# A transformer block on one core: rows behind the second norm turned by VectorE in 32x32 squares instead of by TensorE

## The chip, the cores and the metric

The kernel runs on one core of one Trainium2 chip. A core has five engines that run their own instruction lists and meet at semaphores: TensorE (PE), VectorE (DVE), ScalarE (ACT), GpSimd (POOL) and SyncE (SP, which here only issues DMAs), and 16 DMA engines. The metric is the device time of one execution in microseconds (us), as the median of several.

## The reference

The input is x, 2048 tokens of 1024 features, f32. The block computes

```
u = rmsnorm(x, ln1_g);  proj = u @ w_in            # 2816 columns: a_q a_f a_i a_g | b_q b_k b_v
y_a = hgrn2_mixer(...)                             # 4 heads, gated linear recurrence in chunks of 64
y_b = swa_sink_attention(...)                      # 8 heads, window 128, sinks, ALiBi
h = x + concat(y_a, y_b) @ w_out
u = rmsnorm(h, ln2_g)                              # "the second norm"
h = h + (silu(u @ w_gate) * (u @ w_up)) @ w_down   # 2816 hidden columns
out = rmsnorm(h, final_g)
```

Everything is f32. Precise products are made from pairs: each operand is split into a rounded high part and the rest (`hi`, `lo`), and a product is three matmuls, hi x hi, hi x lo, lo x hi.

## The kernel before

**Mixers.** The tokens are taken in NSB = 4 blocks of T = 512 (`it` = 0 to 3, TB = 4 rows of 128 tokens each). Each engine runs `slots(it)`, 27 slots, and then `out_b(it)`. In slots 0 to 21 TensorE makes one group: 128 columns of `w_in` against u, 8 x 3 matmuls of 128x512 (`group`, L971 to 973). Into the slots a fixed plan puts the small steps: attention step i = 0 to 15 has its scores in slot i+2, its sum in i+3, its turn (`p_turn`) in i+4 and its product with the values in groups of four in slots 8, 12, 16, 20. Recurrence head a has its four groups from slot F_SLOT = (4, 9, 14, 18) on; three slots behind the first come its `iv` turn and key product (`iv_turn`, `keys`), four behind it the turn of its key and the update (`key_turn`, `update`), five behind the output (`output_inside`, L1148, which waits for the last of eight states that VectorE makes in `update`, L1953), six behind the norm. In slots 22 to 26 and in `out_b` TensorE multiplies by `w_out` in units 22 to 29, four k-pairs for the left half of the columns (banks M) and four for the right (banks X). `w_in` and `w_out` are split once, in iteration 0, and stored to `w_scr` as 1 MB units; later iterations load unit n into one of three places (`split`, `split_next`) as soon as unit n-3 has been used (`load_split`, L642). VectorE makes the splits of iteration 0 too (`make_lo`), with GpSimd in some slots.

**The second norm and its turn.** Block it-1's h is kept as four tiles of 128 tokens x 1024 and is scaled in iteration it, slots 12 to 15 (`h_scale`, L2162). The FFN wants it with the features on the partitions. So in slots 18 to 25 of iteration it TensorE turns it, half a row tile (`j` = 0 to 7) a slot: `u_turn` makes four 128x128 transposes into bank X[0] (L1186), ScalarE copies the bank to a tile of four buffers (`u_out`, L1469), and SP stores the tile to `u_scr[it, partition, feature group, token]` (`store_u`, L661). The eight halves of the last block are turned in the FFN, in four pairs behind the products named in `U_LAST`, through X[2] and X[3]. `s_ftr` counts the turns, `s_uev` the copies, `s_us[0..3]` the stores. The rows of x for the residual are loaded over the freed h tiles (`load_rows`, L619), in SP's order `u 3, r 0, r 1, u 4, unit 26, u 5, r 2, u 6, unit 27, u 7, r 3, unit 28, unit 29`; in the last iteration the operand loads stand between these too (`load_operand`, L712).

**FFN.** It is a Strassen-Winograd product over pairs of blocks (NPAIR = 2): operands B11, B21, T1 to T4, B22 are loaded from `u_scr` or combined and split; 22 groups of 7 products of 12 matmuls 128x512 (`ffn_product`, L1282 to 1284), whose weights ScalarE and VectorE split three products ahead (LEAD = 3, L1649 and L2180); and then `down`, 77 rows of 12 matmuls (L1307 to 1309), fed by a ring of four buffers.

**Order around the change.** Every engine works strictly in the order written. SP waits for a semaphore ahead of nearly every DMA, so a late store holds all loads behind it.

Of the kernel before, what the change touches and what calls it, by code (L numbers as in the profile page):

```python
# [94 lines left out]
POOL_LOW = (8, 9, 13, 14, 17, 18, 22)  # L95
COMBINE_AT = {27: 0, 37: 1, 39: 2, 48: 3}
SPLIT_AT = {50: "B11", 52: "T2", 54: "T1", 59: "T3", 61: "B21", 63: "T4", 65: "B22"}
GAIN_AT = (63, 64, 65, 70)
T_LOAD = 9
U_LAST = ((5, 6), (6, 3), (6, 6), (7, 3))  # L100
# [37 lines left out]
def block_program(nc, x, ln1_g, w_in, lb_logits, hgrn_norm_g, attn_sinks, attn_norm_g, w_out, ln2_g,  # L138
# [31 lines left out]
    u_scr = nc.dram_tensor("u_scr", [NSB, P, KD, T], F32, kind="Internal").ap()  # L170
# [6 lines left out]
    with ExitStack() as ctx:  # L177
# [188 lines left out]
        def wait_u_stored(eng, it, j=7):  # L366

            for n in range(4):
                eng.wait_ge(s_us[n], 32 * it + 16 * ((j - n) // 4 + 1))
# [155 lines left out]
        s_ftr = sem("s_ftr")  # L525
# [74 lines left out]
        def _(sp):  # L600
# [12 lines left out]
            def load_rows(it, b):  # L613

                if it == NSB - 1 and b < 2:
                    sp.wait_ge(s_ptr0, NSB * 2 * TB)
                elif it:
                    sp.wait_ge(s_ftr, (it - 1) * 2 * TB + 2 * b + 2)
                sp.dma_start(x_rows(it, b)[:, :], x_t[it * TB + b, :, :]).then_inc(s_xh[b], 16)  # L619
# [37 lines left out]
            def store_u(it, j):  # L657
# [3 lines left out]
                sp.dma_start(u_scr[it, :, 4 * half:4 * half + 4, b * P:(b + 1) * P],  # L661
                             u_tile(it, j)[:, :].rearrange("p (c t) -> p c t", c=4)).then_inc(s_us[j % 4], 16)
# [22 lines left out]
            def load_operand(p, o, part=None):  # L685
# [22 lines left out]
                if p == 0 and o == B22:  # L708
                    sp.wait_ge(s_ftr, (NSB - 2) * 2 * TB + 4)
# [256 lines left out]
        def _(pe):  # L966
# [48 lines left out]
            def group(it, slot):  # L1015
# [5 lines left out]
                for k in range(KD):  # L1021
                    last = product(M[slot % 3][:, :], place_of(it, slot), uhi[:, k, :], ulo[:, k, :], k,
# [144 lines left out]
            def u_turn(it, j):  # L1167

                b, half = divmod(j, 2)
                if it == NSB - 1:  # L1170
                    bank = X[2 + half]
                    pe.wait_ge(s_u, it * TB + j + 1)
                    if j >= 2:
                        pe.wait_ge(s_uev, it * 2 * TB + j - 1)
                    else:
                        pe.wait_ge(s_h, NSB * KD)
                else:
                    bank = X[0]
                    pe.wait_ge(s_u, it * TB + b + 1)
                    if j:  # L1180
                        pe.wait_ge(s_uev, it * 2 * TB + j)
                    else:
                        pe.wait_ge(s_bias, (it + 1) * STEPS + STEPS)
                for c in range(4):
                    k = 4 * half + c
                    last = tr(bank[:, c * P:(c + 1) * P], h_of(it)[b][:, k * P:(k + 1) * P], ident[:, :])  # L1186
                last.then_inc(s_ftr, 1)

            def slots(it):

                for slot in range(SLOTS):
                    if slot < IN_GROUPS and (it or slot >= 2):
                        group(it, slot)
# [36 lines left out]
                    if it and 0 <= slot - UT_SLOT < 2 * TB:  # L1230
                        u_turn(it - 1, slot - UT_SLOT)
# [56 lines left out]
            def ffn(p):  # L1288
                for g in range(NG):
                    for o in range(PRODUCTS):  # L1290
                        ffn_product(p, g, o)
                        if p == 0 and (g, o) in U_LAST:
                            u_turn(NSB - 1, 2 * U_LAST.index((g, o)))
                            u_turn(NSB - 1, 2 * U_LAST.index((g, o)) + 1)

# [58 lines left out]
        def _(act):  # L1354
# [105 lines left out]
            def u_out(it, j):  # L1460
                act.wait_ge(s_ftr, it * 2 * TB + j + 1)
                if j >= 4:
                    act.wait_ge(s_us[j % 4], 32 * it + 16)
                elif it == NSB - 1:
                    act.wait_ge(s_group, NSB * UNITS)
                else:
                    act.wait_ge(s_score, (it + 1) * STEPS + STEPS)
                    act.wait_ge(s_u, (it + 1) * TB)
                A(u_tile(it, j)[:, :], X[0 if it < NSB - 1 else 2 + j % 2][:, :], ACT.Copy).then_inc(s_uev, 1)  # L1469

# [27 lines left out]
            def slots(it):  # L1498
                for slot in range(SLOTS):
# [23 lines left out]
                    if slot in Q_SLOT:  # L1523
# [3 lines left out]
                        elif it >= 2:  # L1527
                            for par in range(2):
                                act.wait_ge(s_us[2 * p + par], 32 * (it - 1))
# [28 lines left out]
                    if it and 0 <= slot - UT_SLOT < 2 * TB:  # L1558
                        u_out(it - 1, slot - UT_SLOT)
# [91 lines left out]
            def ffn(p):  # L1651
                for g in range(NG):
                    G, j = NG * p + g, NJ * p + g // 2
                    x, y, z = banks_of(p, g)
                    for o in range(PRODUCTS):
# [35 lines left out]
                        if p == 0 and PRODUCTS * g + o - 1 in [PRODUCTS * x + y for x, y in U_LAST]:  # L1691
                            for half in range(2):
                                u_out(NSB - 1, 2 * [PRODUCTS * x + y for x, y in U_LAST].index(PRODUCTS * g + o - 1) + half)
# [98 lines left out]
        def _(dve):  # L1792
# [102 lines left out]
            def head_group(it, a, part, bank):  # L1895
# [22 lines left out]
                if part in (1, 2):  # L1918
                    half = slice((part - 1) * (T // 2), part * (T // 2))
                    dve.wait_ge(s_cum, n + 1)  # L1920
                    if a:
# [672 lines left out]
```

## Time and profile before

| | us |
|---|---|
| Median of 3 runs | 2169.23 (2168.64 to 2169.85) |
| The profiled execution's own time | 2167.59 |
| Its span, first to last instruction | 2165.9 |
| TensorE busy | 2134.2 (99%) |
| VectorE busy | 1364.3 (63%) |
| ScalarE busy | 843.6 (39%) |
| GpSimd busy | 432.5 (20%) |
| DMA queue of SP, share of 16 engines | 54.6%, 400.63 MB |

How to read it: a busy TensorE is not TensorE at its peak, since its matmuls overlap and their ends are modelled; the distance from start to start is what a matmul costs. The mixers take from 0 to about 890 us, iterations 1 to 3 some 174 us each, and the rest is the FFN. Idle time of an engine other than TensorE costs nothing by itself.

### The profile page before, as it was taken

How to read it: one execution, taken by the hardware profiler on the slowest of the kernel's cores; microseconds unless marked ns; L12 is line 12 of the kernel's file. 1: busy time of each engine (PE TensorE's matmuls, PEld its weight loads, DVE VectorE, ACT ScalarE, POOL GpSimd, SP SyncE). 2: the span in 40 equal slices, each digit the busy share in tenths (PEclk: the TensorE clock that was granted, in tenths of full speed). 3: DMA queues.
4: the chain of work that ended last, by engine and by line, in shares of the span. 5: the costliest groups of instructions: out<-in, count | busy, mean ns of one | idle time of the engine just before them, and what ended most of it. 6: DMA issues, size and time to landing. Idle time of an engine off the chain costs nothing.

```text
span 2165.9 us, 28872 instructions
## 1 busy us (share of the span) xinstructions
PE 2134.2 (99%) x10708; PEld 1778.9 (82%) x10708; DVE 1364.3 (63%) x2136; ACT 843.6 (39%) x1628; POOL 432.5 (20%) x403
## 2 busy tenths in 40 slices
PE   8999999999999999999999999999999999999998
PEld 7878888888888888788888887888888888888886
DVE  5886477547754776766566765568755556564556
ACT  5343342324232423444333333356433333333445
POOL 2342022102210221222233230000222233210000
PEclk9999999999999999999999999999999999999999
DMA  7666754664467437543355657887433323237666
GB/s 247 227 231 209 264 183 145 198 223 179 146 196 229 171 132 235 217 148 115 107 209 214 218 191 234 261 267 253 172 101 102 106 89 122 93 105 236 225 208 228
DMA packets 215740, 402.48 MB, mean 186 GB/s; under 512 B 16944, under 2 KB 100912, under 8 KB 211760
## 3 DMA queue, kind: packets, MB, share of 16 engines
q1 hardware_dynamic: 215600, 400.63, 54.6%
q8 instruction: 86, 1.41, 0.3%
q14 instruction: 54, 0.44, 0.1%
HBM read 292.04 MB, written 108.53 MB: 185 GB/s over the span
## 4 chain that ended last, share of the span: by engine, by line
PE 87%; DVE 5%; issue 4%; DMA 2%; ACT 1%; POOL 1%; SPq 0%; DVEq 0%; ACTq 0%; POOLq 0%
PE M L1282 10%; PE M L1284 10%; PE M L1283 10%; PE M L971 6%; PE M L973 6%; PE M L972 6%; PE M L1307 3%; PE M L1309 3%; PE M L1308 3%; PE X L1309 3%; PE X L1308 3%; PE X L1307 3%; PE X L1284 3%; PE X L1282 3%; PE X L1283 3%
## 5 line engine op out<-in xcount | busy, mean ns | idle before, releaser
L2292 DVE TENSOR_TENSOR ring_lo<-ring_raw,ring_hi 128x1024 fp32r<-128x1024 f32 x154 | 189.7, 1232 | 162.6 <-ACT ring_hi L1707 162.1
L1707 ACT ACTIVATE ring_hi<-ring_raw 128x1024 fp32r<-128x1024 f32 x154 | 163.3, 1061 | 230.4 <-DMA ring_raw<-a_scr 225.5
L1282 PE MATMUL M<-t_hi,wu_hi 128*128 128x512 f32 x616 | 240.2, 390 | 0.3 <-DVE wu_lo L2180 0.3
L1284 PE MATMUL M<-t_hi,wu_lo 128*128 128x512 f32 x616 | 239.9, 390 | 0.0
L1283 PE MATMUL M<-t_lo,wu_hi 128*128 128x512 f32 x616 | 239.7, 389 | 0.0
L971 PE MATMUL M<-uhi,split 128*128 128x512 f32 (+1 forms) x528 | 206.6, 391 | 2.9 <-DVE ulo L1843 2.9
L973 PE MATMUL M<-uhi,split 128*128 128x512 f32 (+1 forms) x528 | 202.9, 384 | 0.0
L972 PE MATMUL M<-ulo,split 128*128 128x512 f32 (+1 forms) x528 | 202.4, 383 | 0.0
L2180 DVE TENSOR_TENSOR wu_lo<-fraw,wu_hi 128x512 fp32r<-128x512 f32 x132 | 124.0, 948 | 123.3 <-ACT wu_hi L1649 122.9
L2557 POOL TENSOR_TENSOR fs<-fraw 128x512 f32<-128x512 f32 x43 | 61.0, 1418 | 415.8 <-DMA fraw<-in_w_gate_dram 208.5
L2477 POOL TENSOR_TENSOR pr<-pr,rd 128x256 f32<-128x256 f32 x64 | 44.6, 697 | 459.1 <-DVE rd L1854 459.1
L1282 PEld LDWEIGHTS M<-t_hi,wu_hi 128*128 128x128 f32 x616 | 115.6, 188 | 25.0 <-DVE wu_lo L2180 1.1
L1283 PEld LDWEIGHTS M<-t_lo,wu_hi 128*128 128x128 f32 x616 | 115.8, 188 | 24.1
L1284 PEld LDWEIGHTS M<-t_hi,wu_lo 128*128 128x128 f32 x616 | 115.6, 188 | 24.1
L2563 POOL TENSOR_TENSOR fraw<-fraw,fs 128x512 f32<-128x512 f32 x43 | 55.9, 1300 | 369.1 <-DVE wl_lo L2180 369.1
L1307 PE MATMUL M<-ring_hi 128*128 128x512 f32 x308 | 120.4, 391 | 2.3 <-DVE ring_lo L2292 2.3
L1308 PE MATMUL M<-ring_lo,ring_hi 128*128 128x512 f32 x308 | 119.9, 389 | 0.0
L1309 PE MATMUL M<-ring_hi,ring_lo 128*128 128x512 f32 x308 | 119.9, 389 | 0.0
L1307 PE MATMUL X<-ring_hi 128*128 128x512 f32 x308 | 119.8, 389 | 0.0
L1309 PE MATMUL X<-ring_hi,ring_lo 128*128 128x512 f32 x308 | 119.8, 389 | 0.0
L1308 PE MATMUL X<-ring_lo,ring_hi 128*128 128x512 f32 x308 | 119.8, 389 | 0.0
L971 PEld LDWEIGHTS M<-uhi,split 128*128 128x128 f32 x528 | 99.3, 188 | 23.9 <-issue 5.1
(312 smaller groups left out, 5012.6 us busy)
## 6 DMA issues: line engine op xcount, KB each, us to landing
split<-w_scr SPq DMA_DIRECT2D x60, 1024.0 KB, 5.6
ring_raw<-a_scr SPq DMA_DIRECT2D x154, 256.0 KB, 3.6
w_scr<-split SPq DMA_DIRECT2D x30, 1024.0 KB, 6.5
split_next<-w_scr SPq DMA_DIRECT2D x30, 1024.0 KB, 5.0
fraw<-in_w_gate_dram SPq DMA_DIRECT2D x44, 512.0 KB, 4.8
fraw<-in_w_up_dram SPq DMA_DIRECT2D x44, 512.0 KB, 4.8
a_scr<-au SPq DMA_DIRECT2D x88, 256.0 KB, 2.4
ring_raw<-t_scr SPq DMA_DIRECT2D x88, 256.0 KB, 3.0
```

The costliest lines, as they stand in the source:

```text
L971: mm(bank, whi[s][:, kb, :], hi, start=first, stop=False)
L972: mm(bank, whi[s][:, kb, :], lo, start=False, stop=False)
L973: return mm(bank, wlo[s][:, kb, :], hi, start=False, stop=last)
L1282: mm(bank[:, :], wh[:, k, :], hi[:, k, :], start=start and k == 0, stop=False, skip_group_check=True)
L1283: mm(bank[:, :], wh[:, k, :], lo[:, k, :], start=False, stop=False, skip_group_check=True)
L1284: last = mm(bank[:, :], wl[:, k, :], hi[:, k, :], start=False, stop=k == KH - 1, skip_group_check=True)
L1307: mm(bank[:, :], hi[:, 1, tokens], hi[:, 0, :], start=first, stop=False, skip_group_check=True)
L1308: mm(bank[:, :], hi[:, 1, tokens], lo[:, 0, :], start=False, stop=False, skip_group_check=True)
L1309: done = mm(bank[:, :], lo[:, 1, tokens], hi[:, 0, :], start=False, stop=last, skip_group_check=True)
L1707: A(hi[:, :, :], raw_r[:, :, :], ACT.Copy).then_inc(s_rowhi, 1)
L2180: V.tensor_tensor(wl[:, :, :], ffn_part(p, g, o), wh[:, :, :].bitcast(F32), ALU.subtract).then_inc(s_flo, 1)
L2292: V.tensor_tensor(lo[:, :, :], raw_r[:, :, :], hi[:, :, :].bitcast(F32), ALU.subtract).then_inc(s_rowlo, 1)
```

## The change

1. `u_turn` (TensorE) and `u_out` (ScalarE) go. In their slots VectorE makes one `transpose` of a half tile, 128 tokens x 512 features, straight from h (`u_blocks`). It turns each 32x32 square by itself: token 32i+t, feature 32n+c comes to partition 32i+c, column 32n+t.
2. The squares are put in order by the stores. `u_scr` becomes `[NSB, 32, KD, 4, T]`, and `store_u` makes four DMAs, one for each 32 tokens, in runs of 32 tokens, 128 bytes; before it was one DMA with runs of 128 tokens, 512 bytes. The semaphores `s_us` count four times as far. `load_operand` reads rows of T tokens (2048 bytes), as before, in the new order.
3. `s_ftr` goes: the loads into freed h tiles, and of B22, wait for `s_uev`, which VectorE now raises. `out_b` waits for the last scores of bank X[0] and not for the last copy of u.
4. `key_turn` of heads 0 to 2 moves from behind the group of its slot (8, 13, 18) into the middle of it, between k = 3 and k = 4. Head 3's stays in slot 22.
5. On VectorE the reciprocal of the decay (`inverse`, parts 1 and 2 of a head) moves to the front of its slot, ahead of the scores; in slots 5, 9, 13, 17 (`UNFOLD_LAST`) the masked copy of the turned probabilities (`unfold`, L1892) moves behind the head's keys, update and norm.

```diff
-    u_scr = nc.dram_tensor("u_scr", [NSB, P, KD, T], F32, kind="Internal").ap()
+    u_scr = nc.dram_tensor("u_scr", [NSB, P // 4, KD, 4, T], F32, kind="Internal").ap()
...
-                eng.wait_ge(s_us[n], 32 * it + 16 * ((j - n) // 4 + 1))
+                eng.wait_ge(s_us[n], U_PARTS * (32 * it + 16 * ((j - n) // 4 + 1)))
...
                 elif it:
-                    sp.wait_ge(s_ftr, (it - 1) * 2 * TB + 2 * b + 2)
+                    sp.wait_ge(s_uev, (it - 1) * 2 * TB + 2 * b + 2)
...
-                sp.dma_start(u_scr[it, :, 4 * half:4 * half + 4, b * P:(b + 1) * P],
-                             u_tile(it, j)[:, :].rearrange("p (c t) -> p c t", c=4)).then_inc(s_us[j % 4], 16)
+                for i in range(U_PARTS):
+                    tokens = slice(b * P + 32 * i, b * P + 32 * i + 32)
+                    sp.dma_start(u_scr[it, :, 4 * half:4 * half + 4, :, tokens].rearrange("c k m t -> c (k m) t"),
+                                 u_tile(it, j)[32 * i:32 * i + 32, :].rearrange("c (n t) -> c n t", n=16)
+                                 ).then_inc(s_us[j % 4], 16)
...
-                    sp.dma_start(OPERAND[o][2][:, k, :], u_scr[2 * p + n, :, k0 + k, :]).then_inc(s_opl[o], 16)
+                    sp.dma_start(OPERAND[o][2][:, k, :], u_scr[2 * p + n, :, k0 + k, :, :].rearrange("c m t -> m c t")
+                                 ).then_inc(s_opl[o], 16)
...
-            def group(it, slot):
+            def group(it, slot, head=None):
...
                 for k in range(KD):
+                    if head is not None and k == KD // 2:
+                        key_turn(it, head)
...
-                for c in range(4):
-                    k = 4 * half + c
-                    last = tr(bank[:, c * P:(c + 1) * P], h_of(it)[b][:, k * P:(k + 1) * P], ident[:, :])
-                last.then_inc(s_ftr, 1)
...
-                    a = head_at(slot, UPDATE)
-                    if a is not None and slot != OUT_A:
-                        key_turn(it, a)
...
-                        if c == 0 and bank == 0 and it:
-                            pe.wait_ge(s_uev, it * 2 * TB)
+                        if c == 0 and bank == 0:
+                            pe.wait_ge(s_bias, (it + 1) * STEPS)
...
-                A(u_tile(it, j)[:, :], X[0 if it < NSB - 1 else 2 + j % 2][:, :], ACT.Copy).then_inc(s_uev, 1)
...
+                    a, part = head_part(slot)
+                    if part in (1, 2):
+                        inverse(it, a, part)
...
-                        unfold(it, i)
+                        if slot not in UNFOLD_LAST:
+                            unfold(it, i)
...
+                    if slot in UNFOLD_LAST:
+                        unfold(it, step_at(slot, P_TURN))
...
+                    if it and 0 <= slot - UT_SLOT < 2 * TB:
+                        u_blocks(it - 1, slot - UT_SLOT)
...
+            def u_blocks(it, j):
+                b, half = divmod(j, 2)
+                dve.wait_ge(s_u, it * TB + (j if it == NSB - 1 else b) + 1)
+                if j >= 4:
+                    dve.wait_ge(s_us[j % 4], U_PARTS * (32 * it + 16))
+                elif it == NSB - 1:
+                    dve.wait_ge(s_group, NSB * UNITS)
+                else:
+                    dve.wait_ge(s_score, (it + 1) * STEPS + STEPS)
+                    dve.wait_ge(s_u, (it + 1) * TB)
+                V.transpose(u_tile(it, j)[:, :], h_of(it)[b][:, half * T:(half + 1) * T]).then_inc(s_uev, 1)
...
+                        if p == 0 and (g, o) in U_LAST:
+                            for half in range(2):
+                                u_blocks(NSB - 1, 2 * U_LAST.index((g, o)) + half)
```

## Rows read from the trace of the kernel before

**Rows 1.** The page, part 1: busy us, share, instructions of each engine.

```profile
PE 2134.2 (99%) x10708; PEld 1778.9 (82%) x10708; DVE 1364.3 (63%) x2136; ACT 843.6 (39%) x1628; POOL 432.5 (20%) x403
```

**Rows 2.** Waits of TensorE, whole run: us in total, times, longest.

```profile
PE X L1148 <- DVE st L1953: 5.7, 5, 1.8
...
PE X L1124 <- POOL key L2466: 2.8, 3, 2.1
PE X L1141 <- ACT kst L1415: 2.7, 4, 0.7
```

**Rows 3.** Windows: us, busy by engine, PEclk, DMA share, GB/s.

```profile
862.00:884.00 22.00, 21.96 (x99) 17.84 (x97) 17.29 (x12) 8.31 (x6) 0.00 (x0) 1.00 1.05 398
424.00:446.00 22.00, 22.00 (x112) 18.46 (x111) 10.32 (x14) 5.77 (x11) 0.00 (x0) 1.00 0.77 265
```

**Rows 4.** Groups of TensorE by line: busy us, mean ns | idle before.

```profile
L1186 PE MATMUL X<-ident,h 128*128 128x128 f32 x96 | 15.2, 281 | 0.0
...
L1186 PE MATMUL X<-ident,h_last 128*128 128x128 f32 x32 | 4.1, 272 | 0.0
```

**Rows 5.** Timeline of TensorE, iteration 1, slot 22: start, us.

```profile
406.33 0.39 PE L979 MATMUL M<-split,yhi 128*128 128x512 f32 x1
...
406.79 0.39 PE L981 MATMUL M<-split,yhi 128*128 128x512 f32 x1
407.02 0.60 PE L1132 MATMUL X<-ident,forget 128*128 128x128 f32 x4
...
407.69 0.40 PE L980 MATMUL M<-split,ylo 128*128 128x512 f32 x1
```

**Rows 6.** Groups of VectorE by line: a copy of a whole tile.

```profile
L2032 DVE COPY oT<-M 128x512 f32<-128x512 f32 x16 | 11.0, 685 | 3.6 <-PE M L1099 3.6
```

**Rows 7.** Timelines of four engines, iteration 1, slots 13 to 18.

```profile
341.95 1.22 DVE L1892 TENSOR_TENSOR pT<-X,keep 128x1024 int32<-128x1024 int32 x1
...
345.79 0.49 PE L1148 MATMUL X<-iv,amask 128*128 128x128 f32 x2 [0.83 <-DVE st L1953]
...
349.45 0.54 DVE L1900 TENSOR_SCALAR forget<-forget,f_mul,f_add 128x512 f32<-128x512 f32 x1
...
373.84 0.58 ACT L1409 ACTIVATE iv<-X 128x512 f32<-128x512 f32 x1
...
377.74 0.49 PE L1141 MATMUL X<-iv,kst 64*128 64x128 f32 x4 [0.69 <-ACT kst L1415]
```

**Rows 8.** Timeline of all engines, iteration 1, slots 22 and 23.

```profile
412.53 0.35 DVE L1953 SCALAR_TENSOR_TENSOR st<-state,cum,X 128x128 f32<-128x128 f32 x1 [0.46 <-PE X L1141]
...
415.56 1.05 PE L1148 MATMUL X<-iv,amask 128*128 128x128 f32 x8
```

**Rows 9.** Timelines, iteration 0 (slots 7, 8) and iteration 1 (slot 7).

```profile
70.61 1.16 PE L1124 MATMUL X<-qdec,key 128*128 128x128 f32 x8 [2.11 <-POOL key L2466]
...
74.61 0.58 ACT L1409 ACTIVATE iv<-X 128x512 f32<-128x512 f32 x1
...
291.80 0.58 ACT L1409 ACTIVATE iv<-X 128x512 f32<-128x512 f32 x1
```

**Rows 10.** DMA at 124.1 to 126, then 13.0 to 14.6: packets, MB, share.

```profile
q1 hardware_dynamic: 728, 0.37, 71.6%
...
q1 hardware_dynamic: 1788, 0.03, 65.9%
```

**Rows 11.** Timeline of SP, iteration 3: issues of units 26, 28, a tile.

```profile
855.48 0.53 SPq L642 DMA_DIRECT2D split<-w_scr  x1
...
864.21 0.45 SPq L661 DMA_DIRECT2D u_scr<-uthird  x1
...
867.75 0.53 SPq L642 DMA_DIRECT2D split<-w_scr  x1
```

**Rows 12.** DMA issues at 867.6 to 867.9: count, KB, us to landing.

```profile
split<-w_scr SPq DMA_DIRECT2D x1, 1024.0 KB, 10.8
```

**Rows 13.** Timeline of TensorE, iteration 3: the first matmul of unit 28.

```profile
878.63 0.50 PE L979 MATMUL X<-split,yhi 128*128 128x512 f32 x1
```

More of the change, by code:

```diff
@@ L95 @@
 POOL_LOW = (8, 9, 13, 14, 17, 18, 22)
+UNFOLD_LAST = (5, 9, 13, 17)
 COMBINE_AT = {27: 0, 37: 1, 39: 2, 48: 3}
@@ L99 @@
 T_LOAD = 9
+U_PARTS = 4
 U_LAST = ((5, 6), (6, 3), (6, 6), (7, 3))
@@ L524, in block_program @@
         s_fo = sem("s_fo")
-        s_ftr = sem("s_ftr")
         INI, DST = 10, 4
@@ L708, in load_operand @@
                 if p == 0 and o == B22:
-                    sp.wait_ge(s_ftr, (NSB - 2) * 2 * TB + 4)
+                    sp.wait_ge(s_uev, (NSB - 2) * 2 * TB + 4)
                     sp.wait_ge(s_u, (NSB - 1) * TB)
                 for k in range(KH) if part is None else (part,):
-                    sp.dma_start(OPERAND[o][2][:, k, :], u_scr[2 * p + n, :, k0 + k, :]).then_inc(s_opl[o], 16)
+                    sp.dma_start(OPERAND[o][2][:, k, :], u_scr[2 * p + n, :, k0 + k, :, :].rearrange("c m t -> m c t")
+                                 ).then_inc(s_opl[o], 16)
             def store_a(p, j, n):
@@ L1165, in head_turn @@
                 last.then_inc(s_amul, 1)
[L1167 to L1183, printed above, removed]
-                for c in range(4):
-                    k = 4 * half + c
-                    last = tr(bank[:, c * P:(c + 1) * P], h_of(it)[b][:, k * P:(k + 1) * P], ident[:, :])
-                last.then_inc(s_ftr, 1)
             def slots(it):
@@ L1192, in slots @@
                     if slot < IN_GROUPS and (it or slot >= 2):
-                        group(it, slot)
+                        group(it, slot, head_at(slot, UPDATE))
                     for k in A_PLAN.get(slot, ()):
@@ L1229, in slots @@
                             step(it, a)
-                    if it and 0 <= slot - UT_SLOT < 2 * TB:
-                        u_turn(it - 1, slot - UT_SLOT)
             def out_b(it):
@@ L1291, in ffn @@
                         ffn_product(p, g, o)
-                        if p == 0 and (g, o) in U_LAST:
-                            u_turn(NSB - 1, 2 * U_LAST.index((g, o)))
-                            u_turn(NSB - 1, 2 * U_LAST.index((g, o)) + 1)
             def down(p):
@@ L1458, in swa_hi @@
                 A(yhi[:, HEADS + p, :], oT[p][:, :], ACT.Copy).then_inc(s_ybhi, 1)
[L1460 to L1468, printed above, removed]
-                A(u_tile(it, j)[:, :], X[0 if it < NSB - 1 else 2 + j % 2][:, :], ACT.Copy).then_inc(s_uev, 1)
             def h_square(it, b):
@@ L1528, in slots @@
                             for par in range(2):
-                                act.wait_ge(s_us[2 * p + par], 32 * (it - 1))
+                                act.wait_ge(s_us[2 * p + par], U_PARTS * 32 * (it - 1))
                         for par in range(2):
@@ L1557, in slots @@
                             step(it, a)
-                    if it and 0 <= slot - UT_SLOT < 2 * TB:
-                        u_out(it - 1, slot - UT_SLOT)
                     if 0 <= slot - X_SCALE < 2 and it + 1 == NSB:
@@ L1690, in ffn @@
                             h_root(NSB - 1)
-                        if p == 0 and PRODUCTS * g + o - 1 in [PRODUCTS * x + y for x, y in U_LAST]:
-                            for half in range(2):
-                                u_out(NSB - 1, 2 * [PRODUCTS * x + y for x, y in U_LAST].index(PRODUCTS * g + o - 1) + half)
                         if g == NG - 1 and o == S3:
@@ L1917, in head_group @@
                                            op0=ALU.mult, op1=ALU.mult).then_inc(s_qdec, 1)
[L1918 to L1921, printed above, removed]
-                        dve.wait_ge(s_key, 2 * n)
-                    V.reciprocal(cuminv[:, half], cum[w][:, half]).then_inc(s_inv, 1)
                 if part == 3:
@@ L1927, in head_group, with inverse @@
                                            op0=ALU.add, op1=ALU.mult).then_inc(s_gs, 1)
+            def inverse(it, a, part):
+                n = it * HEADS + a
+                half = slice((part - 1) * (T // 2), part * (T // 2))
+                dve.wait_ge(s_cum, n + 1)
+                if a:
+                    dve.wait_ge(s_key, 2 * n)
+                V.reciprocal(cuminv[:, half], cum[a % 2][:, half]).then_inc(s_inv, 1)
             def keys(it, a):
```

## The prediction

> **What bounds the kernel now.** I read first the page's busy shares: TensorE is busy in 99% of the span and VectorE in 63%, so only what takes time off TensorE's queue, or puts a wait into it, moves the end [rows 1]. The second view is TensorE's list of waits over the whole run: about 20 us in all, of which VectorE's state chain, GpSimd's key and ScalarE's `kst` copy hold 11.2 us, all inside the mixers [rows 2]. The third is the DMA share by stretches: where iteration 1 moves its stores of u, from 424 to 446 us, the 16 DMA engines have room (share 0.77), but in the last mixer iteration they are full, at 1.05, from 862 to 884 us [rows 3], and that is where I expect this change to be decided.
>
> **Terms on TensorE.** The change takes 96 + 32 square turns off TensorE [rows 4]. Four turns (of another tile, the same shape) alone between big matmuls are seen from 406.79 to 407.69: from the big matmul before them to the second one behind them 0.90 us pass, where two steps of big matmuls take 0.46 (406.33 to 406.79), so four turns cost 0.44 us [rows 5]. Behind other small matmuls four turns take about the same. 32 groups of four: 32 x 0.44 = **14.1 us gained**. ScalarE's 32 copies of the turned tiles go too; ScalarE is at 39% [rows 1] and no wait of TensorE is for them [rows 2], so that is worth nothing by itself.
>
> **Terms on VectorE.** It gets 32 square turns of 128x512 f32. No such row exists. The nearest are a plain copy of that size, 0.685 us [rows 6], and below it a scalar operation, 0.54; above it stands the masked unfold of 128x1024, 1.22 us [rows 7]. I take 0.7 and keep 0.54 and 1.22 for the range; the difference only delays SP by half a microsecond a tile. The Trainium skill (page "VectorE: DVE Perf Modes", section "The three transpose paths") gives 311 ns for a 128x128 bf16 piece in 32x32 squares, by which four would take an estimated 1.24 us; no run here shows it yet, and by that price VectorE would do 0.5 us more per tile. In slots 18 to 21 the new work falls into VectorE's idle time, since VectorE waits for TensorE in each of them; the last eight lie in the FFN, where VectorE's weights are made three products ahead (LEAD), 36 big matmuls of 0.23 us, 8 us. So the turns themselves cost nothing on the path. Only their lateness does, through SP (below).
>
> In slot 22 the gain is not kept. TensorE does the update first, VectorE then makes eight states one behind the other from 412.53 to 415.56, and TensorE begins L1148 at 415.56, which is to say it already arrives with nothing to spare [rows 8]. With the turn between them gone it arrives 0.4 us sooner and waits 0.4 us longer: **-1.2 us** for three iterations.
>
> **The key's turn and the new order on VectorE.** In slot 14 of each iteration TensorE waits 0.83 us for the last state; VectorE did the unfold (1.22 us) ahead of the states, at 341.95 [rows 7]. With the unfold behind them, and ScalarE's `qs` copy 0.6 us sooner, since `kst` is out of its way, that wait goes; ScalarE and GpSimd behind it have moved by only 0.6, so I count 0.6 x 3 = **1.8 us**. In slot 18 TensorE waits 0.69 us for `kst` [rows 7]. Now the key is turned after half the group, near 373.9, but the turn needs the bank that ScalarE's `iv` copy reads, and that copy runs at 373.84 to 374.42. So a wait of up to 0.6 can take the place of the 0.69. It can also vanish, since the order of VectorE and GpSimd ahead of that copy moves. Bounds 0 and 0.69 x 3; I take **1.4 us**.
>
> Iteration 0 is another matter, since VectorE also splits weights there. The reciprocal now stands ahead of the scores, so in slots 6 and 7 the scores, ScalarE's exponentials and the `iv` copy come up to 1.74 us later. Before, `iv` was copied at 74.61, and TensorE had just lost 2.11 us waiting for the key [rows 9]. After: no wait for the key, TensorE at the half of group 8 at 72.2, `iv` ready near 76.9, then 0.4 for the turn and 2.7 for the second half: 80.1 where it was 77.5 before, -2.6. Against that, the 1.8 us wait of iteration 0 in slot 14 goes; slot 18 costs perhaps 0.7 in the same way. Together **-1.5 us**, between -5 and +5.
>
> **The DMA queue.** A tile of u left in 512 pieces of 512 bytes and now leaves in 2048 pieces of 128, from four issues instead of one. A stretch with only 512-byte packets gives 0.716 x 16 x 1.9 us / 728 = 29.9 ns each; one with 1,788 packets in 0.03 MB, 17 bytes each on average, gives 0.659 x 16 x 1.6 / 1788 = 9.4 ns [rows 10]. So a tile takes 512 x 29.9 / 16 = 0.96 us of all engines now, and after the change between 2048 x 9.4 / 16 = 1.2 and 2048 x 29.9 / 16 = 3.8 us. A straight line between the rows gives 14.5 ns; the tiny packets were reads and these are writes to DRAM, so I take 18 ns: 2.3 us, **1.35 us more per tile**. Four issues of 0.45 us cost SP 1.8 us instead of 0.45 [rows 11]. The loads of operands read the same 2048-byte rows as before and cost nothing new.
>
> In iterations 1 and 2 the stretch of these stores has the engines at 0.77 of full [rows 3], and the next weights have several us to spare. Iteration 3 has not. SP issues the weights of unit 28 at 867.75, they take 10.8 us and land at 878.6, and TensorE begins on them at 878.63 [rows 11 to 13]: it is already held by that load. The engines are full up to there, so whatever is put ahead of that load delays it one for one. Ahead of it, since the load of unit 26 at 855.48, stand three tiles of u (the last at 864.21): + 3 x 1.35 = 4.0. The backlog starts somewhat sooner: TensorE is ahead by four turns and the `kst` wait (2.4 us), VectorE ends its slot 22 at 852.0, turns the fifth tile until 852.7, SP issues it four times until 854.5, and then issues unit 26, 1.0 us sooner than before. Landing: 878.6 - 1.0 + 4.0 = 881.6. TensorE would be there at 878.6 - 2.4 - 3 x 0.44 = 874.9. So **a new wait of 6.7 us** (bounds by the piece's price: 3.4 at 9.4 ns, 11.3 at 29.9 ns). The first FFN weights stand behind it in the same queue and in VectorE's, so it isn't won back.
>
> In iterations 1 and 2 SP issues x's rows of block 3 behind the last tile of u, and TensorE's next turns of x need the bank that they free. They come some 3 us later, and TensorE gets there 3 us sooner (seven turns); I count that as just fitting, at nothing.
>
> **Sum.** 14.1 - 1.2 + 1.8 + 1.4 - 1.5 - 6.7 = 7.9 us. The profiled execution took 2167.6 (span 2165.9 and 1.7 around it), 1.6 under the median of 2169.2: 2159.7 there, **2161.3 us** as a median.
>
> **The rivals.**
> *Small pieces are as dear as large ones* (29.9 ns). Iteration 3 waits 11.3, and in iterations 1 and 2 the row of block 3 and unit 28 come about 2.5 us late each. 14.1 - 1.2 + 3.2 - 1.5 - 11.3 - 5 = -1.7: 2170.9. For it: from 4096 to 512 bytes the price per byte already rises. Against it: a tiny packet takes a third of that. Chance 0.20.
>
> *The stores become the bound* (the other side). If a piece costs twice a 512-byte packet, 60 ns, a tile takes 7.7 us. Iteration 3 waits 878.6 - 1.0 + 20 - 874.9 = 22.8, iterations 1 and 2 some 12 each, after the room of 5 us is used: -32 us, 2200. It decides from about 28 ns per piece up, where the sum is nothing. Chance 0.08. The Trainium skill (page "DMA: Bandwidth & Descriptors", section "Specifications") says that below 512 bytes the engines do a read-modify-write, which would be such a doubling; no store to DRAM in this kernel has pieces under 512 bytes, so no row bears it out or excludes it.
>
> *The transfers are hidden anyway.* If the queue isn't what holds unit 28, only 14.1 - 1.2 + 3.2 - 1.5 = 14.6 is left: 2154.6. For it: a tile's stores could drain while SP is still issuing, beside the loads. Against it: the share of 1.05 and a landing 0.04 us ahead of the matmul. Chance 0.18.
>
> *The key's turn within the group makes waits of its own.* ScalarE's `iv` copy is ready only 0.65 us ahead of the half of group 8 (its copy at 291.80 takes 0.58, and the half is near 293.05) [rows 9]. If the new order makes it 1 us late in slots 8 and 18 of three iterations and iteration 0 loses 5, then 7.9 - 1.4 - 3 - 3.5 = 0: 2169. Chance 0.12.
>
> **How the numbers follow.** The forecast has 0.42 and by itself 2157 to 2166. A change of 0.2%, 4.3 us, is about what a measurement of this kernel can tell from none. Faster by more (under 2164.9): most of the forecast, 0.38, the hidden transfers, 0.18, and 0.06 of the others, 0.62. Within: 0.20, from the dear pieces, the key's waits and the forecast's end. Slower: 0.18, all of the store-bound case and half of the dear pieces. The range, 2153 to 2174, leaves out the store-bound case and the tails.
>
> **What the profile after would show.** L1186's and L1469's rows gone and TensorE's busy time about 14 us lower; a turn of 128x512 on VectorE at 0.7 us; packets under 512 bytes up by 65,536 and their mean share; unit 28's matmuls in iteration 3 behind a wait of 3 to 11 us; the 0.83 us wait in slot 14 gone; a wait of TensorE for `iv` at the half of group 8 in iteration 0. The prediction is wrong if a tile's stores take 5 us or more to land in a quiet stretch, or if iterations 1 and 2 also show TensorE waiting for weights.

## The result and the profile after

The changed kernel takes 2242.77 us (median of 5, 2239.54 to 2244.64), the one before 2169.85 in the same measurement (2168.64 to 2171.34): ratio 1.0338, 95% interval 1.0326 to 1.0350. It is slower by 73 us; 2161.3 with a range of 2153 to 2174 was forecast.

The page of the changed kernel, busy us, share and instructions of each engine, and the packets:

```profile
PE 2144.0 (96%) x10580; PEld 1771.0 (79%) x10580; DVE 1379.6 (62%) x2168; ACT 828.2 (37%) x1596; POOL 427.1 (19%) x403
...
DMA packets 265755, 402.47 MB, mean 180 GB/s; under 512 B 83344, under 2 KB 150928, under 8 KB 261776
```

Against [rows 1], TensorE's 128 turns are gone, but its busy time rose by 9.8 us instead of falling. A busy time that grows with fewer instructions asks for the granted clock. Windows of the changed kernel in iteration 3 (us, busy by engine, granted clock, DMA share, GB/s):

```profile
862.00:884.00 22.00, 12.55 (x43) 10.17 (x44) 7.38 (x4) 0.41 (x1) 0.00 (x0) 0.69 0.57 163
...
890.00:935.00 45.00, 22.33 (x69) 17.29 (x70) 16.74 (x12) 7.18 (x6) 3.58 (x3) 0.69 0.62 181
```

In the stretch of [rows 3] TensorE was busy throughout at full clock; now it is busy for 12.6 of 22 us, and part of that at the lower of its two levels (1.2 instead of 2.4 GHz), behind stretches in which it stood idle. The DMA share *fell*, from 1.05 to 0.57. So a queue that holds TensorE up is not full by the mean over 16 engines. TensorE's waits in the changed kernel (us in total, times, longest):

```profile
PE M L1284 <- DVE ring_lo L2278: 26.4, 27, 2.4
PE X L984 <- DMA split<-w_scr: 16.0, 2, 8.8
PE X L984 <- DMA split_next<-w_scr: 11.3, 1, 11.3
PE M L984 <- DMA split<-w_scr: 10.4, 1, 10.4
PE X L1139 <- ACT iv L1386: 8.2, 3, 3.8
...
PE X L1171 <- DVE sqo L1924: 2.1, 3, 0.7
```

The largest entry of [rows 2] was 5.7 us. An iteration is taken here from the end of one iteration's last product with `w_out` to the end of the next one's. So measured, iteration 0 loses 9.9 us (it ended at 241.0, now at 250.9); iterations 1 and 2 gain 3.7 and 3.8 (217.6 and 217.2 us before: an iteration takes 217 us, and not the 174 of the section on the profile before); iteration 3 up to the first FFN product goes from 213.8 to 257.5, a loss of 43.7; the first FFN gate and up stage gains 4.1; the first down stage loses 34.1 (211.5 to 245.6 from its first product to the next stage). The second half of the FFN is as before to 1.1 us. These are times of single executions, and those can lie some us off their medians: the profiled one of e3_order_only below is 3.2 us above it. Both big losses lie where SP issues the loads of operands from `u_scr`. SP's own timeline of the changed kernel in iteration 3 (start, us it took to issue):

```profile
852.10 4.55 SPq L716 DMA_DIRECT2D t_raw<-u_scr  x4
856.70 2.36 SPq L643 DMA_DIRECT2D split<-w_scr  x1
859.10 13.70 SPq L664 DMA_DIRECT2D u_scr<-uthird  x8
872.85 0.56 SPq L643 DMA_DIRECT2D split<-w_scr  x1
...
906.82 0.56 SPq L643 DMA_DIRECT2D split<-w_scr  x1
...
919.63 10.22 SPq L716 DMA_DIRECT2D b_raw<-u_scr  x4
```

SP needs 13.7 us for the eight stores of two tiles. Before, the two stores of two tiles took 0.60 and 0.37 us (at 845.44 and 848.07). Unit 28 leaves at 906.82, not at 867.75 [rows 11]. In the first down stage, 1400 to 1500 us, the loads of the ring land late; the issues of the kernel before and then of the changed one (count, KB, median us to landing):

```profile
ring_raw<-a_scr SPq DMA_DIRECT2D x37, 256.0 KB, 3.6
```

```profile
ring_raw<-a_scr SPq DMA_DIRECT2D x32, 256.0 KB, 6.3
```

### The profile page after: what moved, and what is told of

Its sections match the earlier page's. It is cut to its first block, busy times and chain, and to the rows that moved or that the text cites. A ratio compares the mean times of both kernels' runs of the same rounds, so it can differ in the third digit from the quotient of the medians.

```text
span 2240.8 us, 28680 instructions
## 1 busy us (share of the span) xinstructions
PE 2144.0 (96%) x10580; PEld 1771.0 (79%) x10580; DVE 1379.6 (62%) x2168; ACT 828.2 (37%) x1596; POOL 427.1 (19%) x403
## 2 busy tenths in 40 slices
DMA packets 265755, 402.47 MB, mean 180 GB/s; under 512 B 83344, under 2 KB 150928, under 8 KB 261776
## 4 chain that ended last, share of the span: by engine, by line
PE 75%; DMA 6%; DVE 6%; issue 5%; SPq 5%; ACT 2%; POOL 1%; DVEq 0%; ACTq 0%; POOLq 0%
PE M L1262 10%; PE M L1264 10%; PE M L1263 10%; PE M L976 5%; PE M L978 5%; PE M L977 5%; DMA ring_raw<-a_scr 4%; PE X L1264 3%; PE X L1263 3%; PE X L1262 3%; PE M L1284 3%; PE M L1285 2%; PE M L1286 2%; PE X L1286 2%; PE X L1284 2%
## 5 line engine op out<-in xcount | busy, mean ns | idle before, releaser
L2463 POOL TENSOR_TENSOR pr<-pr,rd 128x256 f32<-128x256 f32 x64 | 39.3, 615 | 495.1 <-DVE rd L1815 495.1
```

## The experiments

**Theory A.** The new layout [NSB, 32, KD, 4, T] makes the source of each 256 KB operand load `"c m t -> m c t"`, outermost dimension 4, and such a load runs on 4 of the 16 DMA engines. These four back up, SP blocks on them, and every transfer spread over all 16 ends with its share on those four. The Trainium skill has the rule (page "DMA: Bandwidth & Descriptors", section "Why a DMA increments its semaphore by 16 and not by 1"): the engines used are the largest number up to 16 that divides the slowest dimension of both sides. The packets counted in p1_transfers_alone, below, agree with it (4 engines for outermost 4). **Theory B.** The stores in 128-byte pieces are what is slow. **A third cause** for iteration 0: one of the order moves.

### Layout and pieces, taken apart

e1_flat, on the changed kernel:

```
- u_scr [NSB, P // 4, KD, 4, T]
+ u_scr [NSB, KD, 4, P // 4, T]
- store: u_scr[it, :, 4*half:4*half+4, :, tokens].rearrange("c k m t -> c (k m) t")
+ store: u_scr[it, 4*half:4*half+4, :, :, tokens].rearrange("k m c t -> c (k m) t")
- load:  u_scr[2*p+n, :, k0+k, :, :].rearrange("c m t -> m c t")
+ load:  u_scr[2*p+n, k0+k, :, :, :].rearrange("m c t -> (m c) t")
```

> The changed kernel, with the tokens' scratch laid out so that the 32 rows and the four places of a tile follow each other in one dimension of 128, read by operand loads of one outermost dimension of 128; the turns on VectorE, the 128-byte pieces of the stores and all order moves stay. Theory A (an operand load whose outermost dimension is 4 runs on 4 of the 16 DMA engines, and these queues hold up everything behind them): iteration 3 and the first down pair get their 43.6 and 34.1 us back, so about 2165 us (2160 to 2172), and TensorE's waits on the ring in the down pair and for the splits in iteration 3 are gone. Theory B (the small pieces of the stores are what is late): nothing comes back, 2230 us or more.

Measured: **2169.88** us (before, same chip: 2168.93), ratio 1.0007 (0.9998 to 1.0017). The packets of 128 bytes are all still there and 73 us have come back (2242.77 less 2169.88). Theory B is out as the main cause. TensorE's waits in iteration 3, timeline of e1_flat:

```profile
874.35 0.50 PE L984 MATMUL X<-split_next,yhi 128*128 128x512 f32 x1 [2.88 <-DMA split_next<-w_scr]
883.71 0.50 PE L984 MATMUL X<-split,yhi 128*128 128x512 f32 x1 [2.00 <-DMA split<-w_scr]
```

The changed kernel's waits for split weights add up to 37.7 us, all in iteration 3. In e1_flat 5.6 are left in the whole run, 4.9 of them in these two.

e2_flat_old_order, e1_flat with the key's turn, the inverse and the unfolding in their old places:

> As e1_flat, and the key's turn, the inverse and the unfolding of the outer product back in the places that they had before, so the turns on VectorE and the new layout alone. Theory A with the loss of iteration 0 laid to the order moves: about 10 us less than e1_flat, 2155 to 2161 us, and no gap of 4 us at the key's turn in iteration 0. If that loss comes from the turns on VectorE instead: the same as e1_flat. Theory B: 2225 us or more.

Measured: **2165.07**, ratio 0.9980 (0.9971 to 0.9990), 4.8 less than e1_flat where 10 was expected (2155 to 2161): the order moves lose 6.2 us in iteration 0 (its end at 249.6 in e1_flat, at 243.5 here) and give some back later.

e3_order_only, the kernel before with those three moves and nothing else:

> The kernel before, with the order moves alone: the key turned within a group, the inverse first, the unfolding last. If the order moves cost iteration 0 its 10 us: 2176 to 2179 us, with the gaps at the key's turn in iteration 0. If the moves are free by themselves: 2169 us. No theory expects a loss in iteration 3 or the down pairs here.

Measured: **2175.36**, ratio 1.0032 (1.0020 to 1.0044). The order moves cost 6.4 us without any turn on VectorE, just under the expected 2176 to 2179. In the trace, which is 3.2 us above the median, iteration 0 ends at 252.6 instead of 241.0, while iterations 1 and 2 are 0.4 and 0.6 us shorter.

e4_layout_only, the kernel before with the changed layout and nothing else:

```
- u_scr [NSB, P, KD, T];  one store a tile, 512-byte pieces
+ u_scr [NSB, P // 4, KD, 4, T];  four stores of 32 partitions a tile, 512-byte pieces
- load u_scr[2*p+n, :, k0+k, :]
+ load u_scr[2*p+n, :, k0+k, :, :].rearrange("c m t -> m c t")
```

> The kernel before, its turns on TensorE, with only the changed kernel's layout of the tokens' scratch: stores of 512-byte pieces, operand loads of outermost dimension 4. Theory A: the whole loss without any small piece, slower by 65 to 78 us, about 2240 us, with the waits on the ring in the first down pair. Theory B: no loss here, 2168 to 2172 us.

Measured: **2233.42**, ratio 1.0297 (1.0282 to 1.0312): 64.5 us of loss, half a us under the expected 65 to 78, without one small piece and without a turn on VectorE. TensorE's waits in e4_layout_only:

```profile
PE M L1309 <- DVE ring_lo L2294: 24.8, 28, 1.7
PE X L981 <- DMA split<-w_scr: 16.2, 2, 9.4
PE X L981 <- DMA split_next<-w_scr: 8.3, 1, 8.3
```

These are waits of the changed kernel's kinds, for the ring and for split weights. e1_flat and e4_layout_only together show that the loss hangs on the layout with its loads, from both sides. The parts don't quite add up: taking the layout back gives 72.9 us, putting it in alone costs 64.5; beside small pieces and moved instructions it costs more than by itself.

### How many engines, counted and timed

p1_transfers_alone:

```
load n = 2, 4, 8, 16:  tile <- scr.rearrange("(c m) t -> m c t", m=n)     load 128:  tile <- scr
each awaited by a VectorE copy (L93); then eight behind each other; stores in 512 and 128 bytes
```

> A kernel that computes nothing and only moves data on SyncE's queue, each transfer awaited by one VectorE copy before the next starts (its output is not the reference's): 256 KB read from DRAM to 128 partitions in rows of 2048 bytes with an outermost dimension of 2, 4, 8, 16 and 128, three times each; eight such reads behind each other with outermost 4 and with 128; 256 KB stored in pieces of 512 and of 128 bytes; one plain read behind four reads of outermost 4, and behind four of 128. Theory A: the read of outermost 4 lasts 3 us and more longer than that of 128 (32 rows an engine by 97 ns against 8), and the eight reads of outermost 4 take 4 times the eight of 128, near 25 us against 6; outermost 16 is as fast as 128. Theory B: all reads last the same, and the store in pieces of 128 bytes takes several times that of 512. The page counts the completion packets of a transfer too: by A 4 for a read of outermost 4 and 16 for one of 128.

The timeline of VectorE in p1_transfers_alone: the idle time in brackets lasts from SP's first issue to the landing of the last transfer of the step, for outermost 2, 4, 8, 16 and 128 (the second of three rounds); then eight reads of 4 and eight of 128; then a store in 512- and one in 128-byte pieces; at the end a plain read behind four reads of 4, and behind four of 128.

```profile
36.67 0.15 DVE L93 COPY mark<-src 128x1 f32<-128x1 f32 x1 [7.71 <-DMA to_two<-scr]
41.74 0.15 DVE L93 COPY mark<-src 128x1 f32<-128x1 f32 x1 [4.92 <-DMA to_four<-scr]
45.73 0.15 DVE L93 COPY mark<-src 128x1 f32<-128x1 f32 x1 [3.83 <-DMA to_eight<-scr]
49.25 0.15 DVE L93 COPY mark<-src 128x1 f32<-128x1 f32 x1 [3.37 <-DMA to_sixteen<-scr]
52.12 0.15 DVE L93 COPY mark<-src 128x1 f32<-128x1 f32 x1 [2.71 <-DMA to_rows<-scr]
...
97.99 0.15 DVE L93 COPY mark<-src 128x1 f32<-128x1 f32 x1 [22.96 <-DMA many_four<-scr]
106.47 0.15 DVE L93 COPY mark<-src 128x1 f32<-128x1 f32 x1 [8.33 <-DMA many_rows<-scr]
...
140.73 0.15 DVE L93 COPY mark<-src 128x1 f32<-128x1 f32 x1 [2.35 <-DMA pieces<-src]
144.29 0.15 DVE L93 COPY mark<-src 128x1 f32<-128x1 f32 x1 [3.41 <-DMA pieces<-src]
...
164.12 0.15 DVE L93 COPY mark<-src 128x1 f32<-128x1 f32 x1 [13.64 <-DMA other<-scr]
170.35 0.15 DVE L93 COPY mark<-src 128x1 f32<-128x1 f32 x1 [6.07 <-DMA other<-scr]
```

The steps 7.7, 4.9, 3.8, 3.4 follow the outermost dimension. From 16 to 128 it is 3.4 to 2.7, and both use 16 engines by the count below, so this last step has another cause, which no run isolates. One load alone loses only 2.2 us by its outermost 4 (3 and more was expected). Eight behind each other take 23.0 instead of 8.3 us, 2.8 times as long (4 times was expected, near 25 against 6). The plain read behind four of them ends 7.6 us later (13.64 - 6.07): of the 4-byte packets that close a transfer, one an engine (counted below), 12 of the plain read's 16 come by 157.8 and the other four at 163.1 to 163.6, behind those of the four loads. That is the damage in the kernel: not the operand, for which TensorE has no wait among the longest above, but the split weights and the ring's rows behind it. SP's timeline of the same run has the blocked issues, eight of outermost 4 and then eight of 128:

```profile
75.05 11.92 SPq L53 DMA_DIRECT2D many_four<-scr  x8
98.17 3.64 SPq L53 DMA_DIRECT2D many_rows<-scr  x8
```

How busy the 16 DMA engines are shows it too. Windows of p1_transfers_alone (us, busy by engine, granted clock, DMA share, GB/s), within the eight reads of 4 and then the eight of 128:

```profile
80.00:95.00 15.00, 0.00 (x0) 0.00 (x0) 1.00 0.26 102
99.00:104.00 5.00, 0.00 (x0) 0.00 (x0) 1.00 0.94 294
```

A share of 0.26 is about that of 4 full engines among 16. The changed kernel has the same stretches: its DMA share in tenths, in 40 slices from 873.9 to 890.0, with four operand loads issued from 873.92 on (most slices behind 878 stand at 2 or 3):

```profile
DMA  3949999993322224283322283222275265233985
```

The number of engines can also be counted. The trace has 4-byte packets beside the data, and they fall under "under 512 B" on the page. The page of p1_transfers_alone:

```profile
DMA packets 18043, 24.92 MB, mean 128 GB/s; under 512 B 5370, under 2 KB 6394, under 8 KB 18042
```

In the packet records of the single loads there are 2, 4, 8, 16 and 16 of the 4-byte packets for outermost 2, 4, 8, 16 and 128, the same in all three rounds. The total agrees: 5370 less the 4096 pieces of 128 bytes are 1274. One such packet for each engine of a transfer, with as many engines as its outermost dimension up to 16, gives: three single loads each, 3 x (2 + 4 + 8 + 16 + 16) = 138; the eights, 16 x 4 + 16 x 16 = 320; the two last groups, 4 x 4 + 6 x 16 = 112; and 44 other transfers of 16 engines (the first two, 10 stores of pieces, 32 of the output), 704. Together 1274. The kernels have 32 + 24 = 56 operand loads; the page of e1_flat:

```profile
DMA packets 266427, 402.47 MB, mean 186 GB/s; under 512 B 84016, under 2 KB 151600, under 8 KB 262448
```

84016 - 83344 = 672 = 56 x 12: with the flat layout each operand load reports from 12 engines more, 16 instead of 4. The pages after and of e4_layout_only also show no landing time for these 56 loads, while the page before has one (4.5 us for `t_raw`).

e8_four_loads, the changed kernel with its layout, each operand load cut into four:

```
-  dma(OPERAND[o][2][:, k, :], u_scr[2*p+n, :, k0+k, :, :].rearrange("c m t -> m c t"))
+  for m in range(4): dma(OPERAND[o][2][32*m:32*m+32, k, :], u_scr[2*p+n, :, k0+k, m, :])
```

> The changed kernel with its layout of the scratch unchanged, and each load of an operand issued as four, one for each of the outer four, 32 rows each. Theory A (it is the outermost dimension of 4 of the one transfer that matters, on both sides 32 now): as e1_flat, 2166 to 2174 us, and 56 x (4 x 16 - 4) = 3360 more completion packets than in the changed kernel. If the rows' order in DRAM (a row's neighbours 8 KB apart) is what made these loads slow: 2215 us or more, as the addresses read are those of the changed kernel.

Measured: **2184.62**, ratio 1.0072 (1.0058 to 1.0086). The same addresses in DRAM in 58 us less, so their spacing isn't the cause (the rows of neighbouring partitions lie 64 KB apart in this layout, not the 8 KB of the expectation), and its page counts 86704 packets under 512 bytes, 3360 more than after, as worked out. But the time lies 10.6 us above the upper end of what was expected. Its SP timeline in iteration 3 shows what stands against it:

```profile
860.51 7.42 SPq L717 DMA_DIRECT2D b_raw<-u_scr  x16
...
875.39 7.27 SPq L717 DMA_DIRECT2D b_raw<-u_scr  x16
```

Sixteen issues take SP 0.46 us each, four took 2.0 to 2.1 in e1_flat, and unit 27 and 28 wait behind them (TensorE waits 8.6 and 6.3 us for split weights).

### What the small pieces cost by themselves

e5_small_pieces_only and e11_four_stores_512, both on the kernel before, its layout and loads kept:

```
  e5:   for m in range(4): dma(u_scr[..., b*P+32*m : b*P+32*m+32], tile[:, :, 32*m:32*m+32])     128-byte pieces
  e11:  for m in range(4): dma(u_scr[it, 32*m:32*m+32, ...], tile[32*m:32*m+32, ...])            512-byte pieces
```

> The kernel before, its turns on TensorE, its layout and loads of operands as they were; only each store of a tile of tokens is cut into four by tokens, with pieces of 128 bytes in place of 512. If the small pieces make the wait of 3.3 us in iteration 3 that e1_flat and e2_flat_old_order still have: 2172 us, with TensorE waiting near 871 us for the split weights. If that wait comes from VectorE or from the changed layout: 2169 us, no such wait. By rival B of the layout experiments it would be 2230 us.

> The kernel before, each store of a tile of tokens issued as four, of 32 partitions each, its pieces still 512 bytes. e5_small_pieces_only had four issues and 128-byte pieces and cost 6.4 us. If it is the piece that costs: 2169 us, no wait for the split weights near 870 us. If it is SyncE's time to issue three transfers more for each tile (0.46 us each): near 2175 us, the same waits as in e5_small_pieces_only. In between: the two share it, read by the waits.

Measured: e5 **2175.26**, ratio 1.0033 (1.0021 to 1.0046), against 2168.82; e11 **2170.06**, ratio 1.0007 (0.9998 to 1.0016), against 2168.53. It is the piece, not the number of issues. e5 lies 3 us above the 2172 expected, and its wait came later than expected (near 871), at unit 28. Its waits for split weights, from e5's TensorE timeline:

```profile
873.98 0.50 PE L981 MATMUL X<-split_next,yhi 128*128 128x512 f32 x1 [0.28 <-DMA split_next<-w_scr]
884.30 0.80 PE L981 MATMUL X<-split,yhi 128*128 128x512 f32 x1 [4.57 <-DMA split<-w_scr]
```

And the same eight issues in SP's timelines, first e5, then e11:

```profile
846.29 9.31 SPq L662 DMA_DIRECT2D u_scr<-uthird  x8
```

```profile
846.57 4.45 SPq L662 DMA_DIRECT2D u_scr<-uthird  x8
```

In the packet records of e5's trace 65,536 packets of 128 bytes take 13.0 ns on average, those of 512 bytes 29.2. A tile costs all engines 2048 x 13.0 / 16 = 1.66 us where it was 512 x 28.8 / 16 = 0.92 in the trace before, 0.74 more.

### Which order move costs iteration 0

e6_key_in_group and e7_inverse_first, each e2_flat_old_order with one move:

> As e2_flat_old_order, with the key's turn within a group and the two other order moves left out. Theory K (the key's turn in the group waits for the copy of the forget gate's inverse that is not there yet, in iteration 0 above all, where groups begin late): nearly the whole loss of iteration 0, 2169 to 2172 us, gaps of 4 us at the turn. Theory R (it is the inverse on VectorE first, that makes what the turn waits for late): 2164 us or less, gaps under 2 us.

> As e2_flat_old_order, with the inverse first on VectorE and the two other order moves left out. Theory K: 2164 us or less. Theory R: 2168 us or more, with a longer wait at the key's turn in iteration 0.

Measured: e6 **2169.32**, ratio 1.0000 (0.9991 to 1.0009); e7 **2162.51**, ratio 0.9972 (0.9962 to 0.9983). Theory K holds: iteration 0 ends at 249.3 in e6, 5.8 later than the 243.5 of e2, and at 241.5 in e7. Slot 18 of iteration 0, e6, ScalarE's copy and TensorE's turn:

```profile
163.98 0.57 ACT L1386 ACTIVATE iv<-X 128x512 f32<-128x512 f32 x1
...
164.70 1.09 PE L1139 MATMUL X<-ident,forget 128*128 128x128 f32 x4 [3.13 <-ACT iv L1386]
```

and in e7, where the turn stands behind the whole group:

```profile
159.99 0.57 ACT L1389 ACTIVATE iv<-X 128x512 f32<-128x512 f32 x1
...
160.71 0.63 PE L1139 MATMUL X<-ident,forget 128*128 128x128 f32 x4 [0.78 <-ACT iv L1389]
```

In both the turn begins 0.15 us behind the end of the copy: in this slot it is held by `iv` in either place (in the kernel before too, by 0.44 us). Within the group it asks 2.7 us sooner, and the twelve products that covered the wait now stand behind it. Windows of the changed kernel behind its turn at 165.18 show a second price, the lower level of the clock (the column before the DMA share):

```profile
160.00:166.00 6.00, 2.39 (x12) 1.80 (x11) 5.86 (x9) 1.90 (x7) 3.33 (x2) 0.83 0.93 344
166.00:170.00 4.00, 4.00 (x12) 3.14 (x11) 0.14 (x1) 0.60 (x1) 0.61 (x1) 0.50 1.04 392
```

e10_inverse_alone, the kernel before with the inverse first:

> The kernel before with the inverse first on VectorE and nothing else. If the gain of 2.5 us between e2_flat_old_order and e7_inverse_first is the order's own: 2166 to 2167 us. If it comes only with the turns on VectorE: 2169 us.

Measured: **2167.76**, ratio 0.9994 (0.9985 to 1.0004). 1.3 us on the medians, but the interval holds no change: whether the move gains by itself stays open.

### The version that wins

e9_best: the flat layout, the turns on VectorE, the inverse first, and the key's turn in the group and the unfolding last only from iteration 1 on.

```
- group(it, slot, head_at(slot, UPDATE))
+ group(it, slot, head_at(slot, UPDATE) if it else None)     and in iteration 0 the old key_turn
- if slot in UNFOLD_LAST:
+ if it and slot in UNFOLD_LAST:
```

> The flat layout and the turns on VectorE, the inverse first in all iterations as in e7_inverse_first, the key's turn within the group and the unfolding last from iteration 1 on only. Against e7_inverse_first the later iterations gain 0.5 to 1.3 us each as in e1_flat, and iteration 0 keeps its time: 2159 to 2162 us, faster than before by 0.3 to 0.45 per cent. If the key's turn in the group brought nothing in iterations 1 to 3: 2162.5 us.

Measured: **2159.45** (2158.18 to 2161.91) against 2169.03, ratio 0.9958 (0.9946 to 0.9971). Iteration 0 ends at 242.0 again, iterations 1 and 2 gain 4.2 and 3.8 us, iteration 3 loses 2.2, and the first FFN gate and up stage gains 3.4. The loss of iteration 3 has these waits for split weights in it:

```profile
865.32 0.50 PE L984 MATMUL X<-split_next,yhi 128*128 128x512 f32 x1 [2.99 <-DMA split_next<-w_scr]
873.78 0.50 PE L984 MATMUL X<-split,yhi 128*128 128x512 f32 x1 [1.12 <-DMA split<-w_scr]
```

## Why the prediction was wrong

**The step that failed** is the sentence "The loads of operands read the same 2048-byte rows as before and cost nothing new." The rows are the same, the spread over the engines is not. It put the 56 operand loads at nothing without looking at how they would be spread. The edit of the layout alone costs 64.5 us (e4), and taking only this back brings the changed kernel from 2242.77 to 2169.88 (e1). I weighed the change by its packets, size by price, and took "16 engines" as given in every division; the diff had the `m` at the front of the load in plain sight. My rival of slow stores had the right places (late weights in iteration 3) and the wrong transfer; it also would have shown iterations 1 and 2 late, and they gained.

**Turns off TensorE, 14.1.** Where it can be read alone it holds: the FFN stage with its eight groups went from 425.1 to 421.7 us in e1, 3.4 for 8 x 0.44 = 3.5. In an iteration eight groups would give 3.5, or 3.1 with slot 22's loss. e2, without the order moves, gained 3.0 in iteration 2, and slot 22 lost nothing (below), so a group was worth 0.37 us there rather than 0.44. In iteration 1 it gained only 1.2, since 1.3 us of waits for split weights (the longest 0.9) came in, which I had counted at nothing.

**Slot 22, -1.2.** It did not come. From the start of the update (L1141 before) to the start of the output (L1148) iterations 1 to 3 took 4.35 us each and take 4.02, 4.02 and 3.99 in the changed kernel, without a wait, so the turn's time was gained there too. That L1148 began just as the states ended in the kernel before was a coincidence of times and not a wait.

**Turns on VectorE, 0.7 us, at no cost.** The time was right; that the turns cost nothing on the path fits iteration 2 of e2, where TensorE has no wait that it didn't have before. The group of the changed kernel:

```profile
L2132 DVE STREAM_TRANSPOSE u<-h 128x512 f32<-128x512 f32 x16 | 11.2, 703 | 0.0
```

The estimate of 1.24 us from the Trainium skill's figure (page "VectorE: DVE Perf Modes", section "The three transpose paths"), which is for bf16, is too high here.

**Slot 14's wait, +1.8.** It went, and another came a slot later: TensorE waits 0.7 us for `sqo` (L1171, a head's scaled output, which VectorE makes at L1924) in each of iterations 1 to 3, the 2.1 us in the waits above. **Slot 18's, +1.4.** In iteration 1 the stretch from the group's first product to the update took 6.84 us and takes 6.45 in the changed kernel, 0.39 less, where 0.47 was counted. Together these two terms were to bring 1.07 us an iteration; e3, which has the moves alone, gained 0.4 and 0.6.

**Iteration 0, -1.5.** Mis-sized: it lost 9.9 in the changed kernel's trace, and 6.2 is what the order moves make between e1 and e2 (11.6 between e3's trace and the one before). Traces in which iteration 0 runs as before (e4, e5, e11) end it 1.0 to 1.7 us later than the trace before does, so part of the rest is the difference between executions; the remainder stays open. In slot 8 I had `iv` ready near 76.9 and the turn behind it; it was ready at 77.14 and the turn began at 77.29, as worked out. For slot 18 I wrote 0.7 "in the same way" without doing the same sum; there TensorE waited 3.61 us, where it was 0.44 before, and went on at the lower clock. What I had left out is that a turn held by `iv` in its old place is held for 2.7 us more in the new one. The rival of the key's turn had this mechanism, and its loss of 5 in iteration 0 was near. In the other iterations it was wrong (they show no such wait in the changed kernel and one of 0.2 us in e1), and its sum was too: 1 us in two slots of three iterations is 6, not 3, which makes 2172 and not 2169.

**The small pieces, -6.7.** e5 measures 6.4 us for them. The price was 13 ns and not 18, half of the extra time per tile that I had counted (0.74 us for 1.35), and the stage was lost to them all the same, since the load of unit 28 is issued late (877.42 in e5, 867.75 before) behind stores on which SP blocks. So that the size came out is in part luck: one reason was half as large, and the other was missing, since I had SP's issues at 0.45 us each whatever their queue held. The Trainium skill's "DMA: Bandwidth & Descriptors", section "Specifications", has a read-modify-write below 512 bytes. A packet of twice the price, as in my rival, does not show: 13.0 ns against 29.2 for a 512-byte packet, which by the byte is 1.8 times as dear.

With the layout repaired (e1) the kernel takes 2169.88, inside the range but 8.6 above the forecast, and most of that is iteration 0. With iteration 0 spared (e9) it is 2159.45, where the sum without its -1.5 gives 2159.8. That this is so close is in part luck: a group of turns and the order moves were worth less than counted, slot 22 lost nothing, and the price of a small piece was lower.

## What to carry to other kernels

Read the outermost dimension of both sides of every DMA that a diff touches before pricing its packets: here a `rearrange` that brought 4 to the front left 12 of 16 engines without a share of the load, and the price fell on what was queued behind it. A mean DMA share that *falls* while transfers land later was the mark of it, and the count of the smallest packets told the number of engines. And before moving an instruction ahead of others, ask what it waits for where it stands: the work that it passes was that wait's cover.

## What the runs showed of the hardware

- A load issued by SP with outermost dimension 2, 4, 8, 16 or 128 on the DRAM side left 2, 4, 8, 16 and 16 of the 4-byte packets (p1), and eight loads of outermost 4 kept the 16 engines busy to 0.26, eight of 128 to 0.94.
- A load of outermost dimension 4 next to others costs them more than itself: 2.2 us alone, 14.6 for eight in a row, 7.6 for a plain read behind four (p1).
- SP's time to issue a DMA depends on what is queued: eight stores of a quarter tile took 4.45 us in e11, 9.31 in e5, 13.70 in the changed kernel; on empty queues four in 128-byte pieces took 1.96 us (p1).
- A 128-byte packet written to DRAM took 12.6 to 13.0 ns in the kernels and 11.6 in p1, less than half of one of 512 bytes (28.8 before, 27.7 in p1).
- After an idle TensorE of 3.6 us in iteration 0, the next 4 us (166 to 170) ran at a granted clock of 0.50.
